# Prompt attention of a hybrid layer: one head at a time, or two heads side by side on TensorE

## What is computed

```python
scale = NSA_HEAD_DIM ** -0.5
s_c = jnp.einsum('bqkgd,bnkd->bkgqn', qb, kc) * scale          # 31 compressed keys
p_c = masked_softmax(s_c, kc_end[None, :] <= t[:, None])
o_c = jnp.einsum('bkgqn,bnkd->bqkgd', p_c.astype(vc.dtype), vc)
...
p_s = masked_softmax(s_s, (pos_s <= t[:, None])[:, :, None])   # selected keys, causal
o_s = jnp.einsum('bkgqm,bkqmd->bqkgd', p_s.astype(v_sel.dtype), v_sel)
...
p_w = masked_softmax(s_w, mask_w)                              # window keys, causal
o_w = jnp.einsum('bkgqs,bskd->bqkgd', p_w.astype(v_win.dtype), v_win)
return gb[..., 0:1] * o_c + gb[..., 1:2] * o_s + gb[..., 2:3] * o_w
```

## Time and profile before

| | us |
|---|---|
| median of 3 runs | 2271.64 |
| the runs | 2271.64, 2272.09, 2260.56 |
| span of the profiled execution, first to last instruction | 2270.8 |
| prompt attention, from 960 to the copy that ends it | 275.4 |
| TensorE busy, whole span | 1979.7 (87%) |
| VectorE busy, whole span | 978.7 (43%) |
| ScalarE busy, whole span | 719.0 (32%) |
| GpSimd busy, whole span | 612.6 (27%) |

### The profile page before, as it was taken

One profiled execution on the slowest core, in us unless ns is written; L12 is line 12 of the kernel. 1 busy time (PEld: TensorE's weight loads), 2 busy tenths in 40 slices (PEclk: granted clock), 3 DMA queues, 4 the chain that ended last, 5 costly groups with the idle time before them and its releaser, 6 DMA issues. The chain is left out here.

```text
span 2270.8 us, 34792 instructions
## 1 busy us (share of the span) xinstructions
PE 1979.7 (87%) x12926; PEld 1674.2 (74%) x12926; DVE 978.7 (43%) x1707; ACT 719.0 (32%) x1415; POOL 612.6 (27%) x396
## 2 busy tenths in 40 slices
PE   3999969887998987899998696997789769999698
PEld 2999956556997985544444596984369759999698
DVE  2408867884112521056765212432011127777400
ACT  2443333334222310145554122333022233333221
POOL 0344323432442320011212042000024214444243
PEclk8999977787999997769998898999999879999899
DMA  3222222212223235030000321520642212222132
GB/s 98 75 92 83 83 72 84 93 65 75 93 83 100 74 116 149 19 109 1 1 0 22 127 83 65 166 74 0 222 141 100 93 50 90 92 92 92 63 94 95
DMA packets 72618, 189.01 MB, mean 83 GB/s; under 512 B 13574, under 2 KB 35335, under 8 KB 68871
## 3 DMA queue, kind: packets, MB, share of 16 engines
q1 hardware_dynamic: 71526, 186.69, 24.7%
q10 hardware_dynamic: 1024, 1.46, 0.2%
HBM read 170.25 MB, written 22.07 MB: 85 GB/s over the span
## 5 line engine op out<-in xcount | busy, mean ns | idle before, releaser
L244 PE MATMUL up_pp<-h,po_ring 128*128 128x260 f32 x2112 | 256.5, 284 | 16.0 <-DVE up_pad L2411 16.0
L244 PEld LDWEIGHTS up_pp<-h,po_ring 128*128 128x128 f32 x2112 | 256.3, 190 | 16.1 <-issue 16.1
L244 PE MATMUL ssd_pp<-h,ssd_ring 128*128 128x260 f32 x2016 | 250.4, 286 | 20.1 <-DVE ssd_pad L469 16.0
L234 POOL TENSOR_TENSOR po_ring<-po_raw,po_ring 128x1024 fp32r<-128x1024 f32 x76 | 182.7, 2405 | 315.0 <-ACT po_ring L211 270.1
L244 PEld LDWEIGHTS ssd_pp<-h,ssd_ring 128*128 128x128 f32 x2016 | 247.4, 192 | 22.6 <-DVE ssd_pad L469 16.1
L211 ACT CAST po_ring<-po_raw 128x1024 fp32r<-128x1024 f32 x70 | 73.6, 1051 | 261.8 <-PE up_pp L244 128.0
L234 POOL TENSOR_TENSOR ssd_ring<-mixed,ssd_ring 128x1024 fp32r<-128x1024 f32 x42 | 101.4, 2415 | 200.1 <-ACT ssd_ring L211 170.2
L244 PE MATMUL pd_pp<-act_t,po_ring 128*128 128x260 f32 x1056 | 128.5, 284 | 18.8 <-DVE pd_credit L2330 18.8
L244 PEld LDWEIGHTS pd_pp<-act_t,po_ring 128*128 128x128 f32 x1056 | 128.3, 190 | 19.0 <-issue 19.0
L244 PE MATMUL nq_pp<-h,nq_ring 128*128 128x260 f32 x960 | 121.3, 287 | 10.8 <-POOL nq_ring L234 10.8
L244 PEld LDWEIGHTS nq_pp<-h,nq_ring 128*128 128x128 f32 x960 | 118.4, 191 | 11.8 <-issue 11.0
(11 more groups left out here) (406 smaller groups left out, 3502.0 us busy)
## 6 DMA issues: line engine op xcount, KB each, us to landing
po_raw<-in_w_up SPq DMA_DIRECT2D x44, 512.0 KB, 3.4
mixed<-in_w_ssd SPq DMA_DIRECT2D x42, 512.0 KB, 3.3
sm_ring<-in_mem_kv SPq DMA_DIRECT2D x16, 1024.0 KB, 4.8
ms_raw<-in_w_ssd_merge SPq DMA_DIRECT2D x24, 512.0 KB, 3.6
mm_raw<-in_w_mkv_qm SPq DMA_DIRECT2D x24, 512.0 KB, 3.4
nq_raw<-in_w_qk SPq DMA_DIRECT2D x20, 512.0 KB, 3.4
mixed<-in_ssd_state SPq DMA_DIRECT2D x16, 512.0 KB, 3.5
out_s_ssd<-mixed SPq DMA_DIRECT2D x16, 512.0 KB, 2.6
```

The costliest lines, as they stand in the source:

```text
L234: pool.tensor_tensor(self.ring[:, u, 1], self.raw[:, u], self.ring[:, u, 0].bitcast(F32), ALU.subtract).then_inc(self.low, 1)
L244: last = pe.matmul(out(n), self.ring[:, b % 2, wn, k], x[:, xn, chunk + k, part], start=start and k == 0 and wn + xn == 0, stop=stop and k ...
```

## The change

A unit becomes a pair v of two heads hd, one in the lower and one in the upper 64 channels of a column of `qk`. There are 8 pairs, all written out without a loop.

- `score` reads the queries where they lie (no copy to `qs`) and issues the matmuls of the two heads in turn, one to each half of the array's rows. It has seven steps: compressed, tile 3 of branch 0, tile 3 of branch 1, tile 2 of branch 0, tile 2 of branch 1, tile 1 of both, tile 0 of both. The compressed scores go into a slot of `pss` too, and each step waits for the exponentials two steps before, across pairs as well.
- `values` issues the matmuls of the two heads in turn too, one to each half of the array's columns.
- `turn_weights` turns both heads' blocks; the two banks of `pst` now belong to the two heads, so that there is one slot instead of two, and each turn waits for the copy of the one before.
- On VectorE one `tensor_tensor_reduce` for each head, branch and tile adds a mask of the full width, scales by -1/8 and takes the minimum, in place of the three instructions before. ScalarE's exp then takes a scale of -1.
- VectorE scales the weights of both branches, in two portions: `normalize_late` does tiles 2 and 3 (before step 6 is shifted), and `normalize_rest` does tiles 0 and 1 and the compressed weights (after the next pair's compressed step). GpSimd has nothing left to do in the stage.
- `pt` has three slots of two heads, and `pso` has two, so that the copy to `ot` comes two steps into the next pair.

```diff
--- before.py
+++ after.py
@@ -1471,46 +1471,37 @@
...
-    PARTS = 1 + TT
+    PAIRS = KV // 2 * GQ
+
...
+    NS = len(STEPS)
+
+    TURNS = [(0, (2, 3)), (1, (2, 3)), (None, ()), (0, (1,)), (1, (1,)), (0, (0,)), (1, (0,))]
+    NT = len(TURNS)
...
-            "summed", "written", "dve", "pool_ready", "windows"))
...
-            def scale(g, u):
-                v = g * UNITS + u
-                pool.wait_ge(pool_ready, v + 1)
-                for i in range(TT):
-                    w = (i + 1) * P
-                    ins = pool.tensor_tensor(pr[:, u % 2, i, 1, 0:w], pr[:, u % 2, i, 1, 0:w],
-                                             den[:, u % 2, i, 2:3].broadcast_to([P, w]), ALU.mult)
...
+            def score(v, n):
+
+                i, branches = STEPS[n]
+                ch, slot = v // GQ, (v * NS + n) % 2
+                if v * NS + n >= 2:
+                    pe.wait_ge(exped, v * NS + n - 1)
...
+                    w = (i + 1) * P
+                    for m, b in enumerate(branches):
+                        for hd in range(2):
+                            half = slice(hd * HD, (hd + 1) * HD)
+                            mm = pe.matmul(pss[:, slot, hd, m * w:(m + 1) * w], qk[half, v, i * P:(i + 1) * P],
+                                           qk[half, NQ + 2 * b + ch, 0:w], start=True, stop=True)
                 mm.then_inc(scored, 1)
...
+            def turn_weights(v, k):
+
+                b, blocks = TURNS[k]
+                pe.wait_ge(scaled, v * 2 + (1 if k < 2 else 2))
+                if v * NT + k:
+                    pe.wait_ge(evacuated, v * NT + k)
...
+            def values(v, k):
+
+                b, blocks = TURNS[k]
+                ch, slot = v // GQ, (v * NT + k) % SLOTS
...
+                    for hd in range(2):
+                        lo = (b * KV + ch * 2 + hd) * HD
+                        mm = pe.matmul(pso[hd * HD:(hd + 1) * HD, v % 2, kb * P:SEQ], vr[:, kb, lo:lo + HD],
+                                       pt[:, slot, hd, n * P:n * P + w], start=k == 0 and kb == blocks[0],
+                                       stop=k == NT - 1, skip_group_check=True)
                     n += TT - kb
-                if k == EV - 1:
...
+            for n in range(NS):
+                score(0, n)
+            for v in range(PAIRS):
+                for k in range(NT):
+                    if v + 1 < PAIRS:
+                        score(v + 1, k)
+                    turn_weights(v, k)
+                    if k:
+                        values(v, k - 1)
+                values(v, NT - 1)
...
-                for part in range(1, PARTS):
-                    i = TT - part
-                    dve.wait_ge(scored, v * 5 + (part + 1))
-                    blk = pss[:, part % 2, :, i * P:(i + 1) * P]
-                    o(dve.tensor_tensor(blk, blk, c["causal"][:].unsqueeze(1).broadcast_to([P, 2, P]), ALU.add))
-                    o.settle()
-                    o(dve.tensor_reduce(mx[:, i, :], pss[:, part % 2, :, 0:(i + 1) * P], AX_X, ALU.max))
...
+            def shift(v, n):
+
+                i, branches = STEPS[n]
+                w, slot = (i + 1) * P, (v * NS + n) % 2
+                dve.wait_ge(scored, v * NS + n + 1)
+                for m, b in enumerate(branches):
+                    for hd in range(2):
+                        part = pss[:, slot, hd, m * w:(m + 1) * w]
+                        ins = dve.tensor_tensor_reduce(part, part, mask[:, SEQ - w:SEQ], -QK_SCALE, 3.0e38, ALU.add,
+                                                       ALU.min, nb[:, v % 2, hd, i, b:b + 1])
+                ins.then_inc(shifted, 1)
...
+            def normalize(v, tiles):
+
+                part, dn = slice(tiles[0], tiles[-1] + 1), den[:, v % 2, :, tiles[0]:tiles[-1] + 1, :]
+                head = v // GQ * 2 * GQ + v % GQ
+                own = gates[:].rearrange("p t (n r) -> p n t r", r=3)[:, head:head + GQ + 1:GQ, part, :]
                 o(dve.tensor_scalar(dn, dn, 1e-30, None, ALU.max))
                 o.settle()
                 o(dve.reciprocal(dn, dn))
                 o.settle()
-                dve.tensor_tensor(dn, dn, gates[:, :, bass.ds(g * 3 + head * 3, 3)], ALU.mult).then_inc(pool_ready, 1)
...
+                for b in range(2):
+                    for hd in range(2):
+                        for i in tiles:
+                            wt = weights(v, hd, b, i)
+                            ins = dve.tensor_scalar(wt, wt, den[:, v % 2, hd, i, 1 + b:2 + b], None, ALU.mult)
+                return ins
...
+            def normalize_late(v):
+
+                dve.wait_ge(exped, v * NS + 5)
+                normalize(v, (2, 3)).then_inc(scaled, 1)
+
+            def normalize_rest(v):
+
+                dve.wait_ge(exped, v * NS + 7)
+                normalize(v, (0, 1))
+                dve.tensor_tensor(pc[:, v % 2], pc[:, v % 2], den[:, v % 2, :, :, 0:1].broadcast_to([P, 2, TT, NCP]),
+                                  ALU.mult).then_inc(scaled, 1)
...
+            for v in range(PAIRS):
+                shift_compressed(v)
+                if v:
+                    normalize_rest(v - 1)
+                shift(v, 1)
+                sum_compressed(v)
+                for n in range(2, 6):
+                    shift(v, n)
+                normalize_late(v)
+                shift(v, 6)
+            normalize_rest(PAIRS - 1)
 
...
+                if n == 1 and v >= 2:
+                    act.wait_ge(turned, (v - 1) * NT)
...
+                for m, b in enumerate(branches):
+                    for hd in range(2):
+                        ins = act.activation(weights(v, hd, b, i), pss[:, slot, hd, m * w:(m + 1) * w], ACT.Exp,
+                                             scale=-1.0, bias=nb[:, v % 2, hd, i, b:b + 1],
+                                             accum_out=den[:, v % 2, hd, i, 1 + b:2 + b])
                 ins.then_inc(exped, 1)
 
...
+            def evacuate(v, k):
+
+                b, blocks = TURNS[k]
+                n = v * NT + k
+                w = SEQ if b is None else P * sum(TT - kb for kb in blocks)
+                rows = slice(0, NCP if b is None else P)
+                act.wait_ge(turned, n + 1)
+                if n >= SLOTS:
+                    act.wait_ge(valued, n - SLOTS + 1)
+                act.copy(pt[rows, n % SLOTS, :, 0:w], pst[rows, :, 0:w]).then_inc(evacuated, 1)
...
+            for v in range(PAIRS):
+                for k in range(NT):
+                    evacuate(v, k)
+                    if k == 1 and v:
+                        write(v - 1)
+                    if v + 1 < PAIRS:
+                        weigh(v + 1, k)
+            write(PAIRS - 1)
...
```

More of the change, by code:

```diff
@@ L1686, in weigh @@
-                ins.then_inc(scaled, 1)
-            def turn(g, first, last):
-                for u in range(UNITS):
-                    if not (last and u == UNITS - 1):
-                        weigh(*on(g, u), first=first and u == 0)
-            weigh(0, 0, first=True)
-            turn(0, True, False)
-            with dve.Fori(1, GQ - 1) as g:
-                o.enter(g, UNITS * (3 + 2 * TT + 3), 1)
-                turn(g, False, False)
-                o.leave(GQ - 1)
-            turn(GQ - 1, False, True)
+                o(dve.tensor_tensor(dn, dn, own, ALU.mult))
@@ L1720, in evacuate @@
-            def evacuate(g, u, k, first=False):
-                v = g * UNITS + u
-                act.wait_ge(turned, v * EV + (k + 1))
-                if k == 0 and not first:
-                    act.wait_ge(summed, v)
-                w = SEQ if k == 0 else P * len([x for x in BLOCKS if x[0] in GROUPS_T[(k - 1) % len(GROUPS_T)]])
-                rows = slice(0, P) if k else slice(0, NCP)
-                act.copy(pt[rows, k, 0:w], pst[rows, k % 2, 0:w]).then_inc(evacuated, 1)
-            for part in range(PARTS):
-                weights(0, 0, part, first=True)
@@ L1732, in turn @@
-            def turn(g, first, last):
-                for u in range(UNITS):
-                    v = g * UNITS + u
-                    for k in range(EV):
-                        evacuate(g, u, k, first=first and u == 0)
-                        if k < PARTS and not (last and u == UNITS - 1):
-                            weights(*on(g, u), k, first=first and u == 0)
-                    half = slice((u % 2) * HD, (u % 2 + 1) * HD)
-                    act.wait_ge(summed, v + 1)
-                    act.copy(at(ot, g + (u // 2) * GQ)[half, PROMPT], pso[half, :]).then_inc(written, 1)
```

205 lines of the change are left out of this document (67 added, 138 removed).

## The result

The changed kernel takes 2181.39 us (median of 4 runs, 2171.16 to 2182.93), the kernel before 2270.76 beside it: ratio 0.9601, 95% interval 0.9571 to 0.9632. The forecast was 2216 and its range ended at 2193: right direction, gain 35 us too small.

The account below looks back on a forecast made before the run. TensorE was taken to bound the stage by its own issue. First turns at 982, seven periods 171, low clock 8.3 and last pair 19 end it at 1180, 55 us earlier: 2216 us, range 2193 to 2257.

Parts of the forecast that it names:

- What bounds the kernel: Stage before the change: TensorE bounds it by its own issue, 15.8 us a unit against a period of 15.75.
- TensorE's columns and mode changes: TensorE per pair: turns 5.14 us, 20 mode changes 3.4, scores and values by columns; 29.2 us without overlap, 18.9 with full.
- What program order allows: TensorE's alternating matmuls in two halves: 2n records take n + 1 times, so 23.1 us a pair; chance 0.46.
- rival of full overlap: Both array halves always work together: TensorE 18.9 us a pair, VectorE sets about 22.5, time 2197 or 2193; chance 0.18.
- VectorE's sum: VectorE's work per pair after the change: 19.9 us, under TensorE's 23.1.
- dear fused instruction: VectorE's 16 fused instructions cost 0.3 us more each: 2240 us with overlap, 2267 without; chance 0.10.
- Where a wait appears: TensorE waits 1.2 us a pair before score step 1, for the chain through step 6; period 24.4 us.
- The low clock until 1001: Start of the stage: granted clock 0.50 to about 1001 as before, costing 8.3 us.
- The sum: Stage end: 982 + 171 + 8.3 + 19 = 1180, 55 us before 1235.4, so 2216 us.
- Stages behind move forward unchanged: Stages after the changed one keep their length, so its 55 us come off the kernel's time.
- The clock stays low: Clock stays at 0.50: 43 us a pair, all eight pairs give 2340 us, slower than before; chance 0.05.

Follow-up runs that it names:

- e4: Kernel before with only VectorE's parts of the change (fused instruction, all scaling on VectorE), heads one after the other: 2271.8 us, ratio to before 1.0012.
- e3: Changed kernel with all score matmuls in one half of the array's rows and all value matmuls in one half of its columns: 2258.0 us.
- v6: Changed kernel with narrow scalings behind score step 1 and a pair's last values after the next pair's first scores and turns: 2172.1 us, 19.57 us a pair.
- e1: Changed kernel with all score matmuls, compressed ones too, in one half of the array's rows: 2229.2 us; 24.33 us a pair, 37.18 twice.
- e2: Changed kernel with both heads' value matmuls in one half of the array's columns: 2204.6 us, 23.98 us a pair.
- e7: Changed kernel with each group's matmuls issued head after head instead of alternating: 2177.0 us, 21.14 us a pair against 20.67.
- e5: Changed kernel with three VectorE instructions again in place of the fused ones: 2183.0 us, 21.56 us a pair against 20.67.
- v4: Changed kernel with the eight narrow scalings moved behind score step 1 on VectorE: 2171.9 us, again 2171.7; 19.57 us a pair against 20.67.
- v1: Changed kernel with score step 6's fused instructions ahead of the wide scalings on VectorE: 2175.1 us, 20.67 us a pair, as in the changed kernel.
- e9: Changed kernel with only the wide scores in one half of the array's rows, compressed scores still in two: 2204.3 us, 23.44 us a pair.
- v8: Changed kernel with narrow scalings and last values later, and step 6's fused instructions ahead of the wide scalings: 2186.2 us, 22.20 to 23.69 us a pair.

## Why the prediction was right or wrong

- **What bounds the kernel: right.** e4 changed everything on VectorE and moved nothing.
- **TensorE's columns and mode changes: right as a sum.** e3 measured 29.13 us for the sum of 29.2. The 20 changes at 0.17 are in it, but no run shows their price alone.
- **"What program order allows": wrong, and the step that failed.** It took (n + 1) for 2n record times, on the argument that the next head's first record stands behind both of the first. The chip runs both heads in the time of one: 1.06 us for 512 columns, not 1.45. 23.1 us should have been about 19 (the sum for full overlap is 18.9, and v6 shows 19.57 with 0.49 of wait). That two records in one half don't overlap holds (e1, e2); that they hold up the other half's doesn't, with up to four ahead (e7). It is the rival of full overlap, to which I gave 0.18. The Trainium skill ("TensorE: Matmul & The Clock Gate", Part 3) says that matmuls in different tiles of the array run at once and take about one matmul's time; the trace agrees, with 1.06 us for two heads' scores against 1.91 in one half.
- **VectorE's sum: too high, with little effect.** Its 16 fused instructions take about 7.0 us a pair, not 10.0, as reads and starts lie inside the neighbours' durations (0.61 start to start); the scalings 1.93 + 2.99 = 4.9 instead of 6.2. e5 shows what such a difference is worth: 2.8 us more on VectorE costs 0.89 a pair. The full-overlap rival's 22.5, which had VectorE as the bound, was too high for the same reason, and so its 2197 lay 16 us above the result. The dear fused instruction didn't occur: 0.71 us at 512 columns. The halved throughput of which the Trainium skill ("Vector Engine (DVE) Microarchitecture Reference", Points that are easy to get wrong) speaks is for two sources in SBUF that aren't bf16. Here one source is in PSUM, and 0.71 us beside the 0.68 of a plain `tensor_tensor` shows no halving; the case of two SBUF sources wasn't run.
- **Where a wait appears: right in kind, wrong in place.** 1.2 us at score step 1 was forecast; TensorE waits about 1.4 us a pair, most of it (0.95) ahead of the 384-column scores, because `normalize_rest` stands ahead of step 1 on VectorE. I hadn't counted that work as delay for the step behind it. v4 shows the place, and v1 that easing the other gains nothing. That the size is near the forecast is luck.
- **The low clock until 1001: wrong, 7.4 us.** It ended at about 983, 24 us after the first scores, instead of 41. From the first turns to those of the last pair it is 145.6 us, 0.9 over seven periods, where I had 8.3. In the other kernels with the wide scores in two halves it ended 23 to 28 us after the first scores; with them in one half (before, e1, e3, e4, e9) 32 to 41; e1's rose at about 989, between the two times that its expectation named. That is a correlation over executions that each start otherwise, not a shown cause.
- **The sum.** End forecast 1180.3, measured 1140.9. The 39.4 us are seven periods (171 forecast, 144.7 measured: 26.3), the low clock (7.4), first turns at 977.5 instead of 982 (4.5; 1.7 of it an earlier start) and the last pair, 17.8 instead of 19 (1.2). "Stages behind move forward unchanged" held within the spread.
- **The clock stays low: nearly right as a danger.** It didn't happen in the changed kernel's steady part, but it did in e1, e3 and e4 with TensorE busy, and in v8 around waits of 1.69 us.

## What to carry to other kernels

Matmuls that leave half of the array's rows or columns idle are worth pairing: two halves cost little more than one, also for float32, and alternating in the program isn't needed for short groups. Once the leading engine needs much less time, look at what stands ahead of the first step of each chain on the follower engines, in their program order; moving eight small scalings behind one step was worth more (1.10 us a pair) than fusing three instructions into one (0.89). And when no row shows an overlap, don't let an argument about issue order replace the open range between none and full.

## What the runs showed of the hardware that I had not expected

- Float32 matmuls in different halves of rows or of columns overlap fully (1.06 us against 1.91, 0.80 against 1.45), with up to four records of one half ahead of the other's; with eight short ones ahead only in part (1.48 us between 1.01 and 1.90), the other half starting beside the fifth. A record can start ahead of three that stand before it in the program (e7, 0.013 us behind the first).
- The granted clock can fall with TensorE busy all but without a gap (21.91 of 22 us in e1, all the time in e3 and e4): in e1 (37.18 us pairs instead of 24.33), in e3 (32.37 instead of 29.13) and in e4 (a unit of 23.64 instead of 15.75). The cause is open. In v8 and in the changed kernel's last pair it fell around or behind waits of 1.69 and 1.83 us.
- A VectorE scaling in SBUF takes 0.480 us with GpSimd idle and 1.048 beside GpSimd's; durations of neighbouring VectorE instructions overlap by about a quarter (0.61 us start to start for 0.84).
